# Joint attention of a two-network kernel: scores in three f32r passes, two heads to a round

## What is computed

```python
def _attend(q, k, v):
    s = jnp.einsum('bqhd,bkhd->bhqk', q, k).astype(jnp.float32) * (A_QK ** -0.5)
    p = jax.nn.softmax(s, axis=-1).astype(v.dtype)
    return jnp.einsum('bhqk,bkhd->bqhd', p, v)
...
        k_all = jnp.concatenate([ky, kx], axis=1)
        v_all = jnp.concatenate([vy, vx], axis=1)
        ox = _blocked_attention(qx, k_all, v_all) * jax.nn.silu(ax)
        x = x + gate[:, None, :] * (jnp.concatenate([fx, gx, ox], axis=-1) @ w_out[l])
        if l < DEPTH - 1:
            oy = _attend(qy, ky, vy).reshape(b, y.shape[1], A_WIDTH) * jax.nn.silu(ay)
```

## Time and profile before

| | us |
|---|---|
| median of 3 runs | 2172.25 (2172.09 to 2174.44) |
| the profiled execution: time | 2174.57 |
| the profiled execution: span | 2173.2 |
| TensorE busy | 2145.1 (99%) |
| VectorE busy | 997.2 (46%) |
| ScalarE busy | 799.3 (37%) |
| GpSimd busy | 734.5 (34%) |

### The profile page before, as it was taken

The page is one execution under the profiler, slowest core; times in us unless marked ns, Lnnn a source line. Parts: engine busy times, 40 slices in busy tenths (PEclk is TensorE's granted clock), DMA queues, the critical chain, the costliest instruction groups (busy, mean ns, idle before and its releaser), DMA issues.

```text
span 2173.2 us, 30673 instructions
## 1 busy us (share of the span) xinstructions
PE 2145.1 (99%) x12586; PEld 1754.2 (81%) x12586; DVE 997.2 (46%) x1764; ACT 799.3 (37%) x1371; POOL 734.5 (34%) x339
## 2 busy tenths in 40 slices
PE   9999999999999999999999999999999999999999
PEld 8778888888889898888878888887886667886677
DVE  5664555541222333334465555345305673552672
ACT  6445333333333333334443333333225442334531
POOL 3116444455443333333174444443221002232102
PEclk9999999999999999999999999999999999999999
DMA  4103444432322222221034444322110001322002
GB/s 153 40 30 110 145 145 146 144 126 97 107 93 88 82 81 82 78 88 69 35 121 146 145 146 146 135 97 95 59 68 35 1 1 40 110 78 83 1 2 78
DMA packets 57659, 191.53 MB, mean 88 GB/s; under 512 B 8112, under 2 KB 11440, under 8 KB 57264
## 3 DMA queue, kind: packets, MB, share of 16 engines
q1 hardware_dynamic: 46128, 155.82, 20.6%
q10 hardware_dynamic: 11392, 33.75, 4.4%
HBM read 185.35 MB, written 2.10 MB: 86 GB/s over the span
## 4 chain that ended last, share of the span: by engine, by line
PE 88%; DVE 3%; ACT 1%; issue 1%; DVEq 1%; POOL 0%; ACTq 0%; POOLq 0%; DMA 0%
PE ps L180 21%; PE ps L181 21%; PE ps L182 21%; PE ps L2729 4%; PE ps L183 3%; PE ps L185 3%; PE ps L184 3%; PE ps L2761 2%; PE ps L2741 2%; PE ps L1105 2%; PE ps L1139 1%; PE ps L1121 1%; PE ps L2284 0%; PE ps L2250 0%; PE ps L2097 0%
## 5 line engine op out<-in xcount | busy, mean ns | idle before, releaser
L253 POOL TENSOR_TENSOR w_lo<-w_raw,w_hi 128x1024 fp32r<-128x1024 f32 x282 | 682.0, 2419 | 1332.2 <-ACT w_hi L170 1318.0
L170 ACT ACTIVATE w_hi<-w_raw 128x1024 fp32r<-128x1024 f32 x284 | 300.3, 1058 | 539.3 <-DMA w_raw<-in_wstream 539.0
L180 PE MATMUL ps<-h_hi,w_hi 128*128 128x512 f32 x1168 | 464.0, 397 | 2.7 <-DVE w_lo L295 1.8
L182 PE MATMUL ps<-h_hi,w_lo 128*128 128x512 f32 x1168 | 455.0, 390 | 0.0
L181 PE MATMUL ps<-h_lo,w_hi 128*128 128x512 f32 x1168 | 455.0, 390 | 0.0
L180 PEld LDWEIGHTS ps<-h_hi,w_hi 128*128 128x128 f32 x1168 | 219.3, 188 | 50.7 <-DVE w_lo L295 2.0
L182 PEld LDWEIGHTS ps<-h_hi,w_lo 128*128 128x128 f32 x1168 | 219.3, 188 | 46.0
L181 PEld LDWEIGHTS ps<-h_lo,w_hi 128*128 128x128 f32 x1168 | 219.5, 188 | 43.3 <-issue 0.7
L183 PE MATMUL ps<-w_hi,h_hi 128*128 128x256 f32 x416 | 116.6, 280 | 0.0
L185 PE MATMUL ps<-w_hi,h_lo 128*128 128x256 f32 x416 | 115.5, 278 | 0.0
L184 PE MATMUL ps<-w_lo,h_hi 128*128 128x256 f32 x416 | 115.5, 278 | 0.0
(11 more groups left out here) (362 smaller groups left out, 4019.5 us busy)
## 6 DMA issues: line engine op xcount, KB each, us to landing
w_raw<-in_wstream SPq DMA_DIRECT2D x283, 512.0 KB, 3.2
f0mod_rows<-in_wmod ACTq DMA_DIRECT2D x24, 512.0 KB, 4.6
f1mod_rows<-in_wmod ACTq DMA_DIRECT2D x24, 512.0 KB, 4.6
dvS<-dvE SPq DMA_DIRECT2D x64, 32.0 KB, 2.5
out<-x SPq DMA_DIRECT2D x8, 256.0 KB, 3.2
x<-in_x SPq DMA_DIRECT2D x3, 512.0 KB, 6.9
l_dft<-in_dft ACTq DMA_DIRECT2D x4, 384.0 KB, 4.2
l_wuq<-in_wuq ACTq DMA_DIRECT2D x2, 768.0 KB, 6.1
```

The costliest lines, as they stand in the source:

```text
L170: self.A.activation(self.slot(self.w_hi, n), self.slot(self.w_raw, n), ACT.Copy).then_inc(self.w_high, 1)
L180: T.matmul(out, wh, ah, start=start, stop=False)
L182: return T.matmul(out, wl, ah, start=False, stop=stop)
L253: G.tensor_tensor(c.slot(c.w_lo, n), c.slot(c.w_raw, n), c.slot(c.w_hi, n).bitcast(F32), ALU.subtract).then_inc(c.w_low, 1)
```

## The change

- `scores` writes three f32r products into each piece of the scores: high query x high key, low query x high key, high query x low key.
- The high parts of the keys are made by ScalarE (`keys_high`), the low parts by VectorE for heads 0 to 3 (`keys_low` in `vector_heads` and in `Joint.vector`) and by GpSimd for heads 4 to 7. Heads 0 to 2 are split in two pieces during the query jobs, behind `root_job` on ScalarE and between `finish_job` and `sum_job` on VectorE; head 3 and heads 4 to 7 in the first steps of the joint stage, behind the exponentials.
- The queries of the first four heads are split by ScalarE and VectorE during the query jobs; each later head of each block is split by GpSimd (`split_query`: a multiplication by one into f32r, a drain, a subtraction), into four buffers.
- A round is now two heads: TensorE does S(i), S(i+1), T of the first unit of the pair before, V of the pair before that, T of the second unit. A double unit is a round by itself. VectorE copies both units of a pair at the second step of a round. The gates, inverses and low parts are moved to the steps that fit.
- In layer 0 S(0) goes ahead of the last transposes of the heads, S(1) behind them. `S` waits for the low parts instead of for the copies.
- The low and high parts of the attention's result go to `o_hl`, over the queries; the other buffers are placed anew.

```diff
+            if NT <= i < NT + 3:
+                self.joint.keys_high(NT - 2, i - NT, i - NT + 1, 0, SEQ)
+            if i == NT + 2:
+                self.joint.queries_high(0)
+            if i == NT + 3:
+                self.joint.keys_high(NT, 0, 3, SEQ, ALLT)
...
             self.finish_job(i)
+            if NT <= i < NT + 3:
+                self.joint.keys_low(c.V, e.parts_low, i - NT + 1, i - NT, i - NT + 1, 0, SEQ)
...
+        steps = [g[-1] for g in groups] + [n, n + 1]
+        self.turns = {steps[g + 1]: group for g, group in enumerate(groups)}
+        self.values = {steps[g + 2]: group[-1] for g, group in enumerate(groups)}
...
-            if 3 <= i < self.n + 3 and i - 3 in self.of_sum:
-                self.sum_values(i - 3)
-            if 2 <= i < self.n + 2:
-                self.turn_probs(i - 2)
+            group = self.turns.get(i, ())
+            if group:
+                self.turn_probs(group[0])
+            if i in self.values:
+                self.sum_values(self.values[i])
+            if len(group) == 2:
+                self.turn_probs(group[1])
...
-        for lo, head, k0, n in cut:
-            ins = T.matmul(c.flat(2 * (i % 2), lo, n), self.y.qT[:, head, self.cols(b)],
-                           self.y.kT[:, head, k0:k0 + n], start=True, stop=True)
...
+            T.matmul(out, q_hi, k_hi, start=True, stop=False)
+            T.matmul(out, q_lo, k_hi, start=False, stop=False)
+            ins = T.matmul(out, q_hi, k_lo, start=False, stop=True)
...
+    def split_query(self, x):
...
+        G.wait_ge(e.scored.h, self.sc0 + self.heads[x - 4][0] + 1)
+        G.tensor_tensor(hi, raw, c.ones[0:A_QK, :], ALU.mult)
+        G.drain()
+        G.tensor_tensor(y.q_lo[:, head, self.cols(b)], raw, hi.bitcast(F32), ALU.subtract).then_inc(e.queries_split.h, 1)
...
-            if 2 <= i < self.n + 2:
-                self.copy_probs(i - 2)
+            if i == 1:
+                self.keys_low(self.c.V, self.e.parts_low, 7, 3, 4, 0, ALLT)
+            for unit in self.turns.get(i, ()):
+                self.copy_probs(unit)
...
+            if 0 < i <= 4:
+                self.keys_high(NT, 3 + i, 4 + i, 0, ALLT)
```

More of the change, by code:

```diff
@@ L2285, in tensor_heads @@
             ins.then_inc(e.heads_turned.h, 1)
+        if self.turn_bank(self.nj - 1) != self.job_bank(self.nj - 1):
+            self.joint.scores(1)
     def raw(self, i):
@@ L2327, in scalar_heads @@
                 self.joint.exp(0)
+                self.joint.keys_high(NT, 3, 4, 0, ALLT)
             j = i - 2
@@ L2638, in __init__ @@
             self.first.setdefault(b, i)
+        groups = []
+        while not groups or groups[-1][-1] < n - 1:
+            i = groups[-1][-1] + 1 if groups else 0
+            groups.append((i, i + 1) if self.units[i][2] == 1 else (i,))
+        steps = [g[-1] for g in groups] + [n, n + 1]
+        self.turns = {steps[g + 1]: group for g, group in enumerate(groups)}
+        self.values = {steps[g + 2]: group[-1] for g, group in enumerate(groups)}
+        summed = {unit: step for step, unit in self.values.items()}
         self.spreads = {}
@@ L2643, in __init__ @@
             if not self.both:
-                self.spreads[self.last[b] + (3 if b < TT - 1 else 2)] = (b, 7)
+                self.spreads[summed[self.last[b]]] = (b, 7)
                 continue
@@ L2717, in scores @@
         b, hd, heads = self.units[i]
-        T.wait_ge(e.copied_out.h, self.y.co0 + NT + b + 1)
+        last = self.exps[i] - 1
+        if i < 4:
+            T.wait_ge(e.parts_low.h, self.pl0 + max(5, i + 4))
+        else:
+            T.wait_ge(e.queries_split.h, self.qs0 + last - 3 + min(max(last - self.first + 1, 0), 4))
         if i >= 2:
@@ L2733, in turn_probs, with gpsimd @@
+    def gpsimd(self):
+        for x in range(4, len(self.heads)):
+            head = x - self.first + 4
+            self.split_query(x)
+            if 4 <= head < A_HEADS:
+                self.keys_low(self.c.G, self.e.queries_split, head + 4, head, head + 1, 0, ALLT)
     def turn_probs(self, i):
```

73 lines of the change are left out of this document (64 added, 9 removed).

## The result

The changed kernel takes 2176.56 us (median of 9 runs, 2174.99 to 2179.45) against 2172.09 (2170.64 to 2174.44) of the kernel before on the same chip: a ratio of 1.0021, 95% interval 1.0011 to 1.0031. It is slower by about 4.5 us, a little more than a measurement of this kernel can tell from no change. The forecast was 2169.6, a gain of 2.65, with a range up to 2175: wrong in its sign, and the time lies outside the range.

The account below looks back on a forecast made before the run. TensorE, busy for 99% of the span, was taken as the bound, with new waits for VectorE's copies. Gains and losses summed to 2.65 us gained; off the median of 2172.25 that gave 2169.6, own range 2167.9 to 2173.5, wider range 2162.5 to 2175.

Parts of the forecast that it names:

- Scores: Joint stage: with f32r passes a single unit's score costs 1.04 us instead of 1.35, a double's 0.72 instead of 1.03.
- Layer 0, S(7) to S(37): Layer 0's joint rounds: groups of 13.0 us against 13.58, less waits for the norm, gate and inverse: 1.45 gained.
- Layer 1, S(8) to S(30): Layer 1's joint rounds: eleven rounds 0.62 us shorter, nine waits of 0.43 given back: 2.9 gained.
- Start of layer 0: Up to S(7): S(0) no longer waits for the last job's scaling, 0.75 us gained; splits in query jobs, 0.55 lost.
- Start of layer 1: Up to S(8): waits for exp(1), copy(0) and GpSimd's low parts, 2.3 us lost; splits in query jobs, 0.95 lost.
- Ends: Last joint rounds to the projection from k=4: 0.85 us gained in layer 0, 1.8 in layer 1.
- Low part of the result: Joint stage: low_out on VectorE can meet GpSimd's split_query, ten times 0.05 us, 0.5 lost.
- starts dearer still: Case in which the starts of the joint stages cost more than forecast: 2173 to 2175 us, chance 0.05.
- Waits were not shorter as a whole: Rival 1: transposes follow copies by 1.00 us, splits and turning do not meet, clock stays up: 2165.7, chance 0.22.
- copies did hold T back: Rival 2 said VectorE's copies never hold transposes back, TensorE alone counts: 2155.7 us; chance 0.04, half way 0.05.
- no low clock came into the rounds: Rival 3: idle time in layer 0's groups lowers the clock, 1.7 us a stretch; six give 2179.8; chance 0.06.
- passes of 256 columns cost 0.12: Rival 4 said 256-column passes can't hide their weight load (0.19), 13 us more over 64 singles: 2179, chance 0.03.

Follow-up runs that it names:

- undisturbed base: The kernel before, unchanged, profiled twice more, with the full clock over layer 0's first scores: times of 2172.47 and 2171.27 us.

## Why the prediction was wrong, step by step

- **Scores.** The passes are 0.23 and 0.12 apart, as said, with 96 rows too, but a round without a wait takes 5.03 instead of 4.93, 0.52 less than before instead of 0.62. The first pass behind transposes takes 0.31 instead of 0.23; that costs nothing in sum, since the last transpose ahead of it takes 0.03 instead of 0.11 (six take 0.63 instead of 0.71). What was missing is the step into the values: the last matmul ahead of them takes 0.09 more to its successor than it otherwise would. In the kernel before the score paid that (1.39 ahead of values, 1.30 ahead of transposes), and the prediction took the mean of both as the price of a score. In the new order the transposes ahead of the values pay it (0.75), so it was not saved with the scores. The rest is some hundredths in the pair.
- **Layer 0, S(7) to S(37): forecast 1.45 gained, measured 1.35 lost.** The step that failed in size is the group: 13.42 instead of 13.0, six times, 2.5 of the 2.8. Both waits are there: 0.76 and 0.43 in brackets, 0.84 from start to start for the first, where the prediction had 0.87 and 0.45. Of the 0.42 too much, 0.13 and 0.12 are the two pairs of scores and 0.22 is the double's score with its wait (1.39 from 1714.59 to 1715.98): the prediction had 0.72 + 0.45 in its sum, though it took 0.80 for the same score to get the wait; 0.05 less elsewhere. What lies outside the groups, at the norm, the gate and the inverse, cost some 0.3 more than the 2.05 of the forecast. The passes were sized by TensorE's rows of another place, where no transposes and no values stood beside them.
- **Layer 1, S(8) to S(30): forecast 2.9, measured 2.62 to 2.66.** Right, by luck in part, since two errors cancel: the eleven rounds are 5.03 instead of 4.93, 1.1 in all, and there are eight waits of 0.29 to 0.47 (3.1 in all from start to start) instead of nine of 0.43 (3.9).
- **Start of layer 0: forecast 0.75 gained, 0.55 for the splits and 0.4 for the clock lost, in sum 0.2 lost. Measured against the undisturbed base 2.2 to 2.3 lost.** This is the step that failed in kind. S(7) came at 1709.61 in the profile of after and at 1709.37 in the earlier trace rows, and from the first projection on it is 0.5 later, so against the shown profile the term looks nearly right. But that profile held 1.7 us of a low clock over the first scores, which other executions don't have, and I took the gain against it off the median. The prediction even named the stretch, with S(0) and S(1) at 4.0 instead of 2.7, and the 2.3 by which the profiled execution lies above the median, and did not put the two together. Without the splits the stretch from the first projection to S(7) is 0.3 longer than in the undisturbed base and not 0.75 shorter, and the splits cost 1.9 there and not 0.55: 1.0 ahead of S(0), in the query jobs, and 0.9 behind it.
- **Start of layer 1: forecast 2.3 + 0.4 + 0.95 = 3.65 lost from the first projection to S(8).** Measured 4.3 to 4.5 against the undisturbed base, 2.8 to 3.1 against the shown profile. The third profile of the changed kernel, with the full clock there as in the base, loses 3.4, and the forecast without its 0.4 for the clock is 3.25; but the parts differ. The splits ahead of S(0) cost 1.6 to 1.8 (0.95 forecast), S(0) to S(8) lost 1.8 at the full clock (2.3 forecast). The mechanism held: S(3) waits 1.33 for exp(1), T(1) 1.35 for its copy, the turning on GpSimd takes up to twice its time. The waits for the low parts were 0.18 and 0.32, not 0.9 and 0.95, since S(3), S(4) and T(1) were already later; when they were moved ahead, these waits came, 0.59 and 1.48.
- **Ends.** Layer 1 gained 1.1 to 1.2 instead of 1.8. In layer 0, S(37) to the projection from k=4 took 20.2 instead of 20.7, so 0.5 of the 0.85 was gained. It was lost again 82 us later: at the sums over tokens for layer 1, TensorE now waits for VectorE, 0.83 in the shown profile, 0.31 and 0.22 in the other two, with some 0.25 more around it, and in the kernel before it does not. The prediction did not look beyond the projection. Why VectorE is later there stays open; without the splits the wait is still there, but only 0.08 (0.36 with what is around it).

```profile
1897.06 0.61 PE L2581 MATMUL ps<-ones,rows 128*128 128x1 f32 x4 [0.83 <-DVE rows L2514]
```

- **Low part of the result, 0.5 lost:** without the splits the rounds of layer 1 are 0.4 shorter, those of layer 0 the same.
- **Rivals.** None of the four was it. Waits were not shorter as a whole, copies did hold T back, no low clock came into the rounds, and passes of 256 columns cost 0.12. Nearest was the case of starts dearer still, which I gave 0.05 and a top of 2175; but the largest part of the miss, 2.8 of some 7, is layer 0's groups, which no rival named.

By sum: 2.65 forecast, 4.1 to 4.8 lost. The difference of about 7 is 2.8 for layer 0's groups, 2 for layer 0's start, 0.7 for layer 1's start, some 1.5 for the two ends, 0.3 for layer 1's rounds, less the 0.5 forecast for the low parts of the result, whose cost is in the measured rounds. The rest, under 0.5 in either direction, I can't assign: it is as large as the spread between profiles.

## What to carry to other kernels

Where two operations share one buffer, the distance between their starts has a lower bound in the copy between them, here 1.96 to 2.02 us in every kernel. Lay out what stands between each two of them on the engine, and on the copying engine put the copy ahead of anything that nobody waits for yet: a swap of two instructions gave 5 us here, another order of transposes 3.6, ScalarE's start at least 1.3, while the cheaper passes alone gave 8. Look for that bound in the kernel before, too: its transposes over a lone score stood 2.02 apart, at the bound and without a wait in the profile, and so a shorter score could give nothing there. And before a term is taken from a profile that lies above the median, find what that execution had more than the others, and take it out of the base.

## What the runs showed of the hardware

- A first f32r matmul of 512 columns behind plain f32 transposes starts its successor after 0.31 us, the next ones after 0.23; but the last transpose ahead of it takes 0.03 instead of 0.11, so the change of type cost nothing in sum. Behind values the first one takes 0.34.
- The last matmul ahead of the values takes 0.09 more: six transposes of 128x128 take 0.75 behind scores and ahead of values, with f32r or plain scores; they take 0.68 to 0.71 ahead of plain f32 scores and 0.57 to 0.63 ahead of f32r ones.
- The record of a matmul runs on for some 0.16 us after the next could start, and shorter waits than 0.1 have no bracket: transposes held by a copy for 0.25 us (0.37 from the last pass instead of 0.12) showed no wait.
- In identical programs the lower clock came in some executions and not in others, at the same places, behind gaps of over 1 us: granted clock 0.91, 1.00 and 1.00 over 1690 to 1710 in three profiles of before, 1.00, 1.00 and 0.74 in three of the changed kernel; 0.91, 0.91 and 1.00 over 1080 to 1100 in the three of before.
- Beside low parts of 0.68 to 0.95 us on VectorE, GpSimd's operations of 0.45 us took up to 1.01; beside VectorE's other operations they took 0.45.
